# Two gated feed-forward products whose weight blocks start 0 to 224 bytes further on, a different distance for each group of columns

## The reference, cut to what matters

```
def swiglu(x, w_gate, w_up, w_down):
    return (silu(x @ w_gate) * (x @ w_up)) @ w_down

h = h + 0.5 * swiglu(rmsnorm(h, ffn1_norm), ffn1_w_gate, ffn1_w_up, ffn1_w_down)
...   # attention and linear attention on 272 tokens
h = h + 0.5 * swiglu(rmsnorm(h, ffn2_norm), ffn2_w_gate, ffn2_w_up, ffn2_w_down)
```

## Time and profile before

| | before |
|---|---|
| median of 3 runs | 911.59 us |
| profiled execution, span | 911.4 us |
| instructions | 18458 |
| PE busy | 896.9 us, 98% |
| PEld busy | 880.6 us, 97% |
| DVE busy | 642.1 us, 70% |
| ACT busy | 525.5 us, 58% |
| DMA, mean | 173 GB/s |

### The profile page before, as it was taken

How to read it: one execution, slowest core, us unless ns; L and a number is a source line. 1 busy time by engine, 2 the same in 40 slices (tenths; PEclk the granted TensorE clock), 3 DMA queues, 4 the chain that set the end, 5 groups by cost and what they waited for, 6 DMA issues and landing times.

```text
span 911.4 us, 18458 instructions
## 1 busy us (share of the span) xinstructions
PE 896.9 (98%) x7415; PEld 880.6 (97%) x7415; DVE 642.1 (70%) x1108; ACT 525.5 (58%) x869; POOL 4.7 (1%) x11
## 2 busy tenths in 40 slices
PE   8999999999999999999999999999999999999996
PEld 7997999999999999999999999999999999999996
DVE  6999888777557666666675547768669877677553
ACT  6897876676336655444444435545775664544452
POOL 1000000000000000000000000000000000000000
PEclk9999999999999999999999999999999999999999
DMA  9742335255765666555556565554425556665641
GB/s 307 239 166 97 139 121 181 93 186 193 251 189 177 200 204 185 171 173 171 181 174 199 168 177 161 158 169 130 148 70 186 186 185 196 201 194 195 212 138 47
DMA packets 110613, 157.63 MB, mean 173 GB/s; under 512 B 9917, under 2 KB 61249, under 8 KB 110401
## 3 DMA queue, kind: packets, MB, share of 16 engines
q1 hardware_dynamic: 109776, 155.19, 53.2%
q10 hardware_dynamic: 576, 0.73, 0.2%
q0 software_dynamic: 176, 0.53, 0.2%
HBM read 155.37 MB, written 1.05 MB: 172 GB/s over the span
## 4 chain that ended last, share of the span: by engine, by line
PE 90%; DVE 6%; ACT 2%; issue 1%; DMA 1%; SPq 0%; DVEq 0%; ACTq 0%
PE ps L1044 28%; PE ps L1046 28%; PE ps L1045 27%; DVE wl L1817 2%; PE ps L1127 1%; ACT wh L1383 1%; PE ps L1091 1%; DMA X<-d_x 1%; DVE S L2222 1%; PE ps L1301 0%; PE ps L1321 0%; DVE S L2068 0%; PE ps L1259 0%; DVE X L1981 0%; PE ps L1281 0%
## 5 line engine op out<-in xcount | busy, mean ns | idle before, releaser
L1817 DVE TENSOR_TENSOR wl<-raw,wh 128x1024 fp32r<-128x1024 f32 (+2 forms) x291 | 346.2, 1212 | 191.4 <-ACT wh L1383 191.2
L1383 ACT ACTIVATE wh<-raw 128x1024 fp32r<-128x1024 f32 (+2 forms) x291 | 298.2, 1046 | 186.8 <-PE ps L1046 186.3
L1044 PE MATMUL ps<-U,wh 128*128 128x256 f32 (+2 forms) x1392 | 397.5, 286 | 2.3 <-DVE wl L1817 2.3
L1046 PE MATMUL ps<-U,wl 128*128 128x256 f32 (+2 forms) x1392 | 390.9, 281 | 0.0
L1045 PE MATMUL ps<-UL,wh 128*128 128x256 f32 (+2 forms) x1392 | 390.4, 280 | 0.0
L1044 PEld LDWEIGHTS ps<-U,wh 128*128 128x128 f32 (+1 forms) x1392 | 262.2, 188 | 5.3 <-DVE wl L1817 3.2
L1045 PEld LDWEIGHTS ps<-UL,wh 128*128 128x128 f32 (+1 forms) x1392 | 262.5, 189 | 1.6 <-issue 1.0
L1046 PEld LDWEIGHTS ps<-U,wl 128*128 128x128 f32 (+1 forms) x1392 | 262.0, 188 | 0.0
L1044 PE MATMUL ps<-H,wh 128*128 128x256 f32 (+1 forms) x736 | 207.4, 282 | 0.1
L1046 PE MATMUL ps<-H,wl 128*128 128x256 f32 (+1 forms) x736 | 205.4, 279 | 0.0
L1045 PE MATMUL ps<-HLO,wh 128*128 128x256 f32 (+1 forms) x736 | 205.1, 279 | 0.0
(11 more groups left out here) (340 smaller groups left out, 784.2 us busy)
## 6 DMA issues: line engine op xcount, KB each, us to landing
raw<-w_ff SPq DMA_DIRECT2D x64, 512.0 KB, 4.5
raw<-ffn_w_gate SPq DMA_DIRECT2D x88, 256.0 KB, 3.6
raw<-ffn_w_up SPq DMA_DIRECT2D x88, 256.0 KB, 4.5
raw<-ffn_w_down SPq DMA_DIRECT2D x44, 512.0 KB, 4.6
raw<-w_in SPq DMA_DIRECT2D x40, 512.0 KB, 4.0
raw<-w_out SPq DMA_DIRECT2D x16, 512.0 KB, 3.6
raw<-wkv_x SPq DMA_DIRECT2D x8, 512.0 KB, 4.2
raw<-w_in SPq DMA_DIRECT2D x9, 256.0 KB, 3.0
```

What stands on the lines that cost most here:

```text
L1044: e.matmul(out, sh, xh, start=(i == 0 and n == 0), stop=False)
L1046: mm = e.matmul(out, sl, xh, start=False, stop=(over and n == nk - 1))
L1383: e.activation(wh, raw, ACT.Copy).then_inc(*up("w_hi", v))
L1817: lo = e.tensor_tensor(wl, raw, wh.bitcast(F32), ALU.subtract)
```

## The change

A table `PLACE` gives each group of `sw1` and `sw2` a number of float32 columns, and `first_columns` adds it to the first column of every block of the group. In bytes: group 0 gets 0, group 1 64, group 2 128, group 3 192, group 4 32, group 5 96, group 6 160, group 7 224, group 8 16, group 9 48, group 10 8. No instruction, wait, transfer or order is changed; all three engines address the blocks by the same function. The longest unit then ends at column 1144 of 1152.

```
+PLACE = {(name, g): n for name in ("sw1", "sw2") for g, n in enumerate((0, 16, 32, 48, 8, 24, 40, 56, 4, 12, 2))}
+
+
 def first_columns(name, g, i):
...
-    return at
+    return [c + PLACE.get((name, g), 0) for c in at]
```

## The result

The changed kernel takes 919.14 us (median of 20 runs, 918.39 to 928.61), the kernel before, run beside it, 913.22 us (20 runs, 911.25 to 920.85). The ratio is 1.0067, 95% interval 1.0047 to 1.0087: slower by 0.67%, 6.1 us. Six of the 20 executions of the kernel before took 917 to 921 us and six 912.7 to 914.0, so its median lies 2 us over its lowest time; from lowest to lowest the difference is 7.1 us. The profiled executions differ by 5.7 us, 917.1 against 911.4 (a span is some 1.8 us shorter than the time of its execution wherever a run has both, so the traced execution of the kernel before took some 913.2 us and not its median of 911.6).

A forecast was written before the change was run, and what follows sets the result against it. TensorE's matmul steps were taken to bound the kernel. Terms of 4.3 (sw2), 2.2 (sw1) and 0.3 us (around them) gave 6.8 on 911.59, so 918.4, shaded to 918.0 us; range 912.8 to 923.5.

The forecast's parts named there:

- The bound: Whole kernel: TensorE busy 98% of the span, so every ns on a matmul's step is paid unless it fills a wait.
- sw2, the three distances with a row: sw2 groups 1, 3 and 4 (128, 0, 96 bytes): 0.54, 0.48 and 0.64 us from trace rows, together 1.7.
- sw2, five without: sw2 groups at 192, 160, 224, 32 and 112 bytes, no trace row: +4.5 ns a matmul, 2.2 us.
- sw2, the two near ones: sw2 groups 8 and 10, 16 and 8 bytes off: half the slow step's excess each, together 0.4 us.
- sw1: sw1 groups 1 to 10: +2.5 ns a matmul in eight far groups, 1.2 in two near ones, 2.2 us.
- Around them: dn1, dn2 and the ten changes of group: 0.3 us, since a steady step can outlive its cause.
- Only some distances cost: Rival: distance modulo 128 or closeness to 64 counts; 192, 72, 80 free, sw1 neutral on average; 915.0 us; chance 0.24.
- Uneven starts: Rival: in both products, loads from blocks off a 64-byte multiple cost 10 ns more; 929.6 us; chance 0.10.
- Nothing moves: Rival: load and stream don't disturb each other; steps differ by how a stretch was entered; 911.6 us; chance 0.09.
- Faster: Rival: sw1's 3.4 ns excess is a clash at 64 that most other distances avoid; 910.0 or 908.3 us; chance 0.07.
- Distance: For each load: start of the weight tile loaded, less start of the activation tile streamed meanwhile, modulo 256 bytes.

The follow-up runs named there:

- the reversed kernel: The changed kernel with its table reversed, groups 1 to 10 at 8, 48, 16, 224, 160, 96, 32, 192, 128 and 64 bytes; 918.30 us.
- The scans: TensorE alone, no reference computed: 96 matmuls at each distance, in 4-byte steps over both scans, then 48 at 64; 113.3 to 123.3 ns with 256 columns.
- the pairs: TensorE alone, two matmuls in turn, each tile's own weights and the other's at different distances; seven of eight mixed cases 116.7 ns, one 118.3.
- the 32-byte test: TensorE alone, 256 columns: low weights and low tile moved by 32 bytes; 118.9 ns together, 118.8 tile alone, 117.8 weights alone.
- the sw2-only kernel: Only sw2's ten groups moved, sw1 left as in the kernel before; 919.91 us against 914.25, ratio 1.0026.

## Why the prediction was right

Forecast 918.0 us, slower; measured 919.1, and 0.67% against a forecast 0.70%. That the two percentages lie so close is in part luck: inside the two products the traces show 7.1 us against the 6.5 forecast for them (4.3 + 2.2), and the spread of the kernel before took over 1 us off the difference of the medians. By its steps:

- *The bound.* Right: no wait appeared, the splits kept 1.05 and 1.22 us, and the whole difference is in the steps of two products.
- *sw2, the three distances with a row.* Forecast 0.54, 0.48 and 0.64 us, measured 0.50, 0.64 and 0.38; together 1.7 and 1.5. A step read over three to nine matmuls gave the size, not the order of the three.
- *sw2, five without.* Forecast 2.2, measured 2.5. The 4.5 ns were a choice between 0 and 13 without a row; measured were 3.4 to 6.7 ns. It was a lucky choice, and 192 had 0 in the reversed kernel.
- *sw2, the two near ones.* The term that was mis-sized: half a slow step each, 0.4 us, because 8 and 16 bytes are near. They cost 0.53 and 0.48, as much as any: 1.0. The scans show why: there is no neighbourhood, 60 and 68 bytes are as bad (119.6, 118.3).
- *sw1.* Forecast 2.2, measured 2.1, with the sizes shared out otherwise: 96 and 72 bytes cost 0.04 and 0.03 us, the eight others 0.19 to 0.29. That 96 is good with 272 columns and dear with 256 was not to be seen before.
- *Around them.* Forecast 0.3; dn2 stayed fast and lost nothing. The worry was right in kind: a slow step does outlive its cause, for sw2 and dn2 whole in the kernel moved by 8 bytes. After group 10 it didn't happen in the traces. In 192's group of the changed kernel it did, 117.8 where the scan and the reversed table have 113.3: 0.43 us.
- *Rivals.* "Only some distances cost" fails by 72 and 80, dear in every trace of a moved sw2 (192 cost in one order and nothing in the other), and by sw1, which lost 2.1 us. "Uneven starts" fails by distance 0, which starts on 64 bytes and is among the dearest. "Nothing moves" fails in all ten groups of both products of the changed kernel; its part on the entry holds at 64, 96 and 192. "Faster" needed a clash of sw1's own at 64; the scan has no distance below its 123.3 ns.
- The Trainium skill's SBUF — State Buffer, section "Who interferes with whom", has moving operand and weight load on independent ports. Against the sum of 0 that the prediction drew from it stands TensorE working alone at 113.3 to 123.3 ns a matmul with only addresses and order changed. Which reads meet, if any do, no run shows.

What the explanation lacks is the mechanism. The prediction took the cause to be how the load meets the tile streamed meanwhile. In sw1 and sw2 a group's weights lie at one distance from every tile (but at a unit's end in sw1), so the forecast would be the same for any pairing of weights and tile, and its coming true is no evidence for this one. "Distance" orders the numbers in uniform streams; the pairs and the 32-byte test show that neither the load against the one tile streaming meanwhile, nor a matmul's weights against its own tile, is enough to give the step.

## What to carry to other kernels

When PE is busy all the time, read the step between starts, stretch by stretch, before looking for waits: equal matmuls at full clock differed by 6% here (113.3 and 120.0 ns). Where blocks of weights and tiles start, against each other, is a parameter to be measured in a scan of TensorE alone, at 4-byte resolution, for the real column count and after several predecessors; no rule of nearness or alignment came out of the scans. Moving all tiles but the constants by 8 bytes put two later products into a slow steady step, so compare steps by product after any edit to the layout, look at the granted clock of both traces, and compare medians only over many runs.

## What the runs showed of the hardware that I had not expected

- A steady second step without a cause in its own stretch: 1530 matmuls at 117.8 ns, at a distance that steps at 113.3 in the kernel before. In TensorE-only streams 64 fell into it after 11 of 16 predecessors.
- Some steady steps recur: 47 of the scans' 64 distances step within 0.12 ns of 113.3, 116.7, 117.8, 118.3 or 120.0 ns with 256 columns, and 47 of 64 near 123.3, 124.4, 125.0 or 126.7 with 272.
- The same kernel's executions group at 911 to 912, 913 to 914 and 917 to 921 us. The middle group goes with a lower mean granted clock. All four traced executions with a mean of 0.996 have a stretch at half clock between 11.7 and 16.3 us, and sw1 begins in them at 350.2 to 351.2 us where it begins at 348.9 to 349.2 in the four traces without the stretch. No trace of the middle group was set beside one of the lowest group for the same kernel, so this is a reading across kernels. The last group, 6 us and more above the lowest, is open. The slow step in sw2 and dn2 is worth 6.8 us (124.45 + 62.19 against 120.01 + 59.84), but it can't be the whole answer: the changed kernel and the sw2-only kernel, whose sw2 is at other distances in ten groups of eleven, have executions 6.8 and 8.5 us above their lowest (925.2 and 924.9), and the kernel moved by 8 bytes, which pays the slow step already, has two 6.6 and 8.6 us above its own (924.7 and 926.7).
